# The first norm of a conditioned decoder trunk, by halves of the features

## The reference

```python
ada = jax.nn.silu(c) @ w_ada[l] + b_ada[l]
sh1, sc1, gt1, sh2, sc2, gt2 = jnp.split(ada[:, None, :], 6, axis=-1)
h = rmsnorm(x, norm1_g[l]) * (1.0 + sc1) + sh1
z = h @ w_in          # 1024 x 8192, then split into q, k, v, gates ...
```

## Time and profile before

| | us |
|---|---|
| median of 3 runs | 2022.48 |
| lowest and highest | 2020.64, 2023.28 |
| the profiled execution, its own time | 2021.04 |
| its span on the core | 2019.2 |
| TensorE busy in the span | 1995.1 |
| VectorE, ACT, POOL busy | 1158.5, 851.8, 183.2 |

### The profile page before, as it was taken

One profiled execution on the slowest core, in us unless ns is written; L12 is line 12 of the kernel. 1 busy time (PEld: TensorE's weight loads), 2 busy tenths in 40 slices (PEclk: granted clock), 3 DMA queues, 4 the chain that ended last, 5 costly groups with the idle time before them and its releaser, 6 DMA issues. The chain is left out here.

```text
span 2019.2 us, 35092 instructions
## 1 busy us (share of the span) xinstructions
PE 1995.1 (99%) x14624; PEld 1898.5 (94%) x14624; DVE 1158.5 (57%) x1814; ACT 851.8 (42%) x1155; POOL 183.2 (9%) x217
## 2 busy tenths in 40 slices
PE   6999999999999999999999999999999999999998
PEld 3879999999998999999989898999999999999998
DVE  5525566774446674646465455767735467646463
ACT  4124444665224244434431354456642333526252
POOL 0001120000032100000220011100000410000004
PEclk9999999999999999999999999999999999999999
DMA  9523243222253232323712314422222622322222
GB/s 362 188 75 108 91 160 97 77 82 86 83 210 145 84 123 87 136 84 126 275 64 69 110 65 145 130 85 81 82 83 84 250 69 84 105 70 99 84 90 105
DMA packets 79067, 233.91 MB, mean 116 GB/s; under 512 B 7376, under 2 KB 27856, under 8 KB 78544
## 3 DMA queue, kind: packets, MB, share of 16 engines
q1 hardware_dynamic: 57312, 206.99, 29.4%
q10 hardware_dynamic: 21616, 24.93, 3.8%
HBM read 219.80 MB, written 12.09 MB: 115 GB/s over the span
## 5 line engine op out<-in xcount | busy, mean ns | idle before, releaser
L1737 PE MATMUL acc<-h_hi,weight_h 128*128 128x288 f32 x1920 | 567.4, 298 | 0.0
L1737 PE MATMUL acc<-h_hi,weight_l 128*128 128x288 f32 x1920 | 560.3, 295 | 0.0
L1737 PE MATMUL acc<-h_lo,weight_h 128*128 128x288 f32 x1920 | 560.2, 294 | 0.0
L505 ACT ACTIVATE weight_h<-raw 128x1024 fp32r<-128x1024 f32 x188 | 199.2, 1060 | 609.9 <-PE acc L1737 513.1
L1737 PE MATMUL acc<-b_hi,weight_l 128*128 128x288 f32 x1520 | 429.5, 295 | 0.0
L1737 PE MATMUL acc<-b_hi,weight_h 128*128 128x288 f32 x1520 | 429.5, 295 | 0.0
L1737 PEld LDWEIGHTS acc<-h_hi,weight_h 128*128 128x128 f32 x1920 | 358.7, 188 | 5.3 <-issue 3.4
L1737 PEld LDWEIGHTS acc<-h_lo,weight_h 128*128 128x128 f32 x1920 | 358.5, 188 | 0.8
L1737 PEld LDWEIGHTS acc<-h_hi,weight_l 128*128 128x128 f32 x1920 | 358.4, 188 | 0.0
L1737 PE MATMUL acc<-b_lo,weight_h 128*128 128x288 f32 x1264 | 356.5, 294 | 0.0
L1068 DVE TENSOR_TENSOR weight_l<-raw,weight_h 128x1024 fp32r<-128x1024 f32 x176 | 227.3, 1292 | 224.1 <-ACT weight_h L505 223.6
(11 more groups left out here) (295 smaller groups left out, 3128.2 us busy)
## 6 DMA issues: line engine op xcount, KB each, us to landing
raw<-stream SPq DMA_DIRECT2D x290, 512.0 KB, 3.5
ada_raw<-ada_in SPq DMA_DIRECT2D x48, 512.0 KB, 6.4
first_raw<-ada_in SPq DMA_DIRECT2D x36, 512.0 KB, 14.5
s_s<-state_in ACTq DMA_DIRECT2D x8, 1024.0 KB, 6.8
ret_s_out<-s_s ACTq DMA_DIRECT2D x8, 1024.0 KB, 4.4
two_raw<-ada_in SPq DMA_DIRECT2D x12, 512.0 KB, 11.0
tables<-const_in SPq DMA_DIRECT2D x2, 1246.0 KB, 13.1
x<-x_in ACTq DMA_DIRECT2D x1, 2304.0 KB, 13.2
```

What stands on the lines that cost most here:

```text
L505: A(weight_h[:, j % 2, :], raw[:, (j + 2) % 4, :], ACT.Copy).then_inc(h_split, 1)
L1737: last = M(acc[j % 2][:, half, 0:HALF], w, r[:, k, half * HALF:(half + 1) * HALF], start=(k == order[0] and n == 0), stop=(k == order[-1] ...
```

## The change

- **x.** Its load moves from ACT's queue, where it was fourth, to the head of SP's queue, before the adaLN tiles.
- **Modulation groups by feature halves.** The host arranges the first sixteen adaLN tiles so that pair 0 holds shift and scale of features 0 to 511, and pair 1 those of features 512 to 1023. POOL writes both segments of a half in one operation. Groups 0 to 2 stay in the buffers that they had; the tiles of group 3 go to the unused slots of `weight_h` and `weight_l` (`early_raw`), since `h_lo` is written before they are used.
- **The norm by halves** (`first_norm`, `first_high`). VectorE multiplies x with the spread root first. ACT then makes `h_hi` as scale times it plus shift, and in a second pass the same sum unrounded into `tmp`; VectorE subtracts. The operations of the samples are split into two halves of the features each.
- **TensorE.** `first_mean` moves from the middle of group 1 into the middle of group 0 (behind its tile j = 1). `spread_root(0)` goes ahead of `turn(0)`. Group 3 and `turn(1)` move into `first_pair`: `on_high(0, 0)`, group 3 with `on_high(1, 0)` behind its first tile, the low parts of the first half for tile 0, `turn(1)`, the same for tile 1, then the second half, in which `on_high(1, 4, 2)` and `on_high(1, 6, 2)` take two feature tiles each. The number of matmuls is the same.

The diff, cut to its core:

```diff
@@ SP's queue
+            sp.dma_start(x[:], x_in).then_inc(x_loaded, 16)
             for n in range(ADA_PROLOGUE):
-                load_into(n, first_raw[n], first_loaded[n])
+                load_into(n, early_raw[n], first_loaded[n])
@@ ACT
-            act.dma_start(x[:], x_in).then_inc(x_loaded, 16)
...
+            def first_high(half):
+                act.wait_ge(ada_ready, half + 1 + 2)
+                if half:
+                    act.wait_ge(scales_ready, 1)
+                else:
+                    act.wait_ge(first_samples, GAINS_A)
+                for m in range(4 * half, 4 * half + 4):
+                    act.wait_ge(xn_ready, m + 1)
+                    A(prompt(one(h_hi, m)), prompt(one(tmp, m)), ACT.Identity, bias=column(ada, m), scale=column(scale1, m)).then_inc(h_rounded, 1)
+                for m in range(4 * half, 4 * half + 4):
+                    act.wait_ge(h_rounded, m + 1)
+                    A(prompt(one(tmp, m)), prompt(one(tmp, m)), ACT.Identity, bias=column(ada, m), scale=column(scale1, m)).then_inc(scaled, 1)
...
-                    act.wait_ge(scales_ready, 1)
-                    for m in range(KT):
-                        if m == 6:
-                            ada_row_out(1)
-                        scale_tile(m, scale1)
+                    first_high(0)
+                    ada_row_out(1)
                     ada_sum_out(1)
-                    act.wait_ge(ada_ready, 2 + 2)
-                    high(0, 0)
+                    first_high(1)
@@ VectorE
+                def scale_and_shift(half):
...
+                    dve.wait_ge(ada_ready, half + 1 + 2)
+                    gains_done, scaled_done = ((first_samples, GAINS_A), (first_samples, SCALED_A)) if half == 0 else ((scales_ready, 1), (s_scaled, 2))
+                    V.scalar_tensor_tensor(scale1[:, rows, :], ada[:, KT + 4 * half:KT + 4 * half + 4, :], 1.0, gb, ALU.add, ALU.mult).then_inc(gains_done[0], 1)
...
+                    V.tensor_tensor(cols(tmp), cols(tmp), of_half(scale1), ALU.mult).then_inc(scaled_done[0], 1)
...
+                    V.tensor_tensor(cols(h_hi), cols(tmp), of_half(ada[:, 0:KT, :]), ALU.add).then_inc(first_samples, 1)
...
+                    V.tensor_tensor(cols(tmp), cols(tmp), of_half(ada[:, 0:KT, :]), ALU.add).then_inc(sum_done[0], 1)
...
+                    last = V.tensor_tensor(samples(h_lo)[:, rows], samples(tmp)[:, rows], samples(h_hi)[:, rows].bitcast(F32), ALU.subtract)
...
+                def normal(half):
+                    for m in range(4 * half, 4 * half + 4):
+                        V.tensor_tensor(prompt(one(tmp, m)), prompt(one(x, m)), spread_p, ALU.mult).then_inc(xn_ready, 1)
+                def first_low(half):
+                    for m in range(4 * half, 4 * half + 4):
+                        dve.wait_ge(scaled, m + 1)
+                        V.tensor_tensor(prompt(one(h_lo, m)), prompt(one(tmp, m)), prompt(one(h_hi, m)).bitcast(F32), ALU.subtract).then_inc(h_ready, 1)
+                dve.wait_ge(spread, 1)
+                V.tensor_tensor(samples(tmp), samples(x), spread_s.unsqueeze(1).to_broadcast([128, KT, 2, HALF_S]), ALU.mult).then_inc(s_scaled, 1)
+                normal(0)
+                scale_and_shift(0)
+                normal(1)
+                first_low(0)
+                scale_and_shift(1)
+                first_low(1)
@@ POOL, add_bias
+                if p < 2:
+                    at_half = lambda t: t.rearrange("p (s h q) c -> p s h q c", s=2, h=2)[:, :, p, :, :]
...
+                    G.tensor_tensor(at_half(ada[:, 0:2 * KT, :]), ada_sum[:].rearrange("p (s q) c -> p s q c", s=2), at_half(both), ALU.add).then_inc(ada_ready, 1)
+                    return
@@ TensorE, first_pair
+                if n == 0:
+                    on_high(0, 0)
+                    ada_group(3, 0, early_raw[3], first_loaded[3], lambda: on_high(1, 0), 0)
+                    on_low(0, range(4))
+                    turn(1)
+                    on_low(1, range(4))
+                    on_high(0, 4)
+                    on_high(1, 4, 2)
+                    on_low(0, range(4, KT))
+                    on_high(1, 6, 2)
+                    on_low(1, range(4, KT))
+                    return
@@ TensorE, before first_pair
-                    ada_group(0, 0, first_raw[0], first_loaded[0])
-                    ada_group(1, 0, first_raw[1], first_loaded[1], first_mean)
+                    ada_group(0, 0, first_raw[0], first_loaded[0], first_mean)
+                    ada_group(1, 0, first_raw[1], first_loaded[1])
+                    spread_root(0)
                     turn(0)
-                    spread_root(0)
                     ada_group(2, 0, first_raw[2], first_loaded[2])
-                    ada_group(3, 0, first_raw[3], first_loaded[3])
-                    turn(1)
@@ the host
+    by_half = [w_ada[0][seg][4 * half:4 * half + 4] for half in range(2) for seg in range(2)]
+    w_ada = np.concatenate(by_half + [w_ada[l][seg] for l, seg in ADA_ORDER[2:]])
```

More of the change, by code:

```diff
@@ L50 @@
 ADA_SUMMED = (0, 1, 4, 10)
+GAINS_A, SCALED_A, HIGH_A, SUM_A, HIGH_B = range(1, 6)
 NORM_SHIFT = [ADA_ORDER.index(pair) + 1 for pair in ((0, 0), (0, 3), (1, 0), (1, 3))]
@@ L192, in build @@
                                  for g, home in ((1, "b_hi"), (2, "b_lo"), (3, "h_lo"), (4, "h_hi"))]
+        early_raw = first_raw[0:3] + [[place(f"early_raw{q}", [128, 1024], F32, offs[home] + slot * 4096)
+                                       for q, (home, slot) in enumerate((("weight_h", 2), ("weight_h", 3), ("weight_l", 2), ("weight_l", 3)))]]
         x_part = place("x_part", [128, 2, NB_S], F32, offs["side"] + 4608)
@@ L1085, in shift_samples @@
             def shift_samples(n, shift_at):
-                if n == 0:
-                    V.tensor_tensor(by_sample(h_hi), by_sample(tmp), to_samples(ada[:, shift_at:shift_at + KT, :]), ALU.add).then_inc(first_samples, 1)
-                    dve.wait_ge(first_samples, 1)
                 V.tensor_tensor(by_sample(tmp), by_sample(tmp), to_samples(ada[:, shift_at:shift_at + KT, :]), ALU.add).then_inc(xn_ready, 1)
             def low(n, shift_at):
[L1094 to L1098, removed]
+                dve.wait_ge(h_rounded, rounded(n))
                 V.tensor_tensor(samples(h_lo), samples(tmp), samples(h_hi).bitcast(F32), ALU.subtract).then_inc(h_ready, 1)
@@ L1136, in _ @@
                     root(0)
[L1137 to L1140, removed]
+                    first_norm()
                     dve.wait_ge(tables_loaded, 16)
@@ L1779, in first_mean @@
             def first_mean():
+                pe.wait_ge(const_loaded, 16)
                 pe.wait_ge(squares_ready, 1)
@@ L1791, in first_pair, with on_high @@
                 pe.wait_ge(acc_free, lay * LAYER_TILES + off + 2)
-                def on_high(j, first):
-                    for k in range(first, first + KT // 2):
+                def on_high(j, first, count=KT // 2):
+                    for k in range(first, first + count):
                         if j == 0:
                             pe.wait_ge(h_rounded, rounded(n) + k)
-                        if n == 0 and k == 0:
-                            pe.wait_ge(first_samples, 1)
+                        if n == 0 and j == 0 and k % 4 == 0:
+                            pe.wait_ge(first_samples, (HIGH_A, HIGH_B)[k // 4])
                         for w in (weight_h, weight_l):
@@ L1802, in on_high, with on_low @@
                                 M(acc[j][:, half, 0:HALF], w[:, j, k * 128:(k + 1) * 128], h_hi[:, k, half * HALF:(half + 1) * HALF], start=(k == 0 and w is weight_h), stop=False)
-                def on_low(j):
-                    for k in range(KT):
+                def on_low(j, steps=range(KT)):
+                    for k in steps:
                         if j == 0:
@@ L1810, in on_low @@
                             last = M(acc[j][:, half, 0:HALF], weight_h[:, j, k * 128:(k + 1) * 128], h_lo[:, k, half * HALF:(half + 1) * HALF], start=False, stop=(k == KT - 1))
-                    last.then_inc(tile_done, 1)
+                    if k == KT - 1:
+                        last.then_inc(tile_done, 1)
+                if n == 0:
[10 more added lines that the diff above has]
+                    return
                 on_high(0, 0)
@@ L1821, in _, with ada_group @@
             for lay in range(DEPTH):
-                def ada_group(n, loads, slots=ada_raw, loaded=ada_loaded, between=None):
+                def ada_group(n, loads, slots=ada_raw, loaded=ada_loaded, between=None, after=1):
                     p, odd = n // 2, n % 2
@@ L1834, in ada_group @@
                         last.then_inc(ada_used, 1)
-                        if j == 1 and between is not None:
+                        if j == after and between is not None:
                             between()
```

31 lines of the change are left out of this document (23 added, 8 removed).

## The result

Before 2022.09 us (22 runs, 2020.64 to 2024.34), after 2025.65 us (22 runs, 2024.98 to 2026.88): ratio 1.0018, interval [1.0012, 1.0024]. The change makes the kernel 3.6 us slower, clear of the noise and less than the 0.2% that I called telling. The forecast was 2023.2, in a range of 2019.3 to 2026.0. The profiled executions differ by more, 2019.2 and 2023.6 us of span: 4.4 us.

What follows compares the result with a forecast made beforehand. TensorE, 99% busy, was taken as the bound from tile 2 on, so prologue moves carry to the end: 2021.04 + 0.75 = 2021.8, by the median 2023.2 us; range 2019.3 to 2026.0.

Steps and rivals of the forecast that it cites:

- x is early, and it helps nothing: Start: x is there by 8.7 us, 7 us earlier, but the squares end at 17.9, only 0.8 us earlier.
- ACT's queue is held by turns: Start: queues alternate by packet, so c arrives about 8.5 us and `small` about 9.9 instead of 7.0, bounds 7.0 to 10.9.
- The mean: TensorE's mean matmuls: start at 17.9 us, partly at 1.2 GHz, take 6.05 us, end at 23.95 instead of 26.12.
- rival (E): Mean ends at 25.6 us, from `small` at 10.9 and 5.4 us at 1.2 GHz: +2.4 us, 2024.9; chance 0.12.
- (D): Start: `small` lands at 13.2 us or later, ACT's queue getting still fewer turns; loss passes 4 us; chance 0.04.
- The path from e: From the mean's end to tile 0's end: 23.45 us, so tile 0 ends at 47.4 us against 46.66.
- The hand-over: Between tile 0's end and tile 2: only 16 matmuls cover preparing `weight_l`, so TensorE idles 1.8 us.
- The order of group 3: In `first_pair`: the last adaLN tile waits for `on_high(1, 0)`, so the second turn comes 4 us later.
- rival (C): Clock falls to 1.2 GHz in a pause from e+6.5 to e+18.2: +4 to +11 us, 2027 to 2033; chance 0.05.
- The sum: Whole kernel: tile 2 starts at 51.4 instead of 50.64 us, +0.75 us, giving 2021.8, by the median 2023.2 us.
- my offset of 1.44 us: Whole kernel: profiled execution 2021.04 us against median 2022.48; the difference is added to the forecast.
- (A): Start: ACT's queue isn't held up, `small` lands at 7.0 us, e at 21.1: -2.1 us, 2020.4; chance 0.2.

Runs made afterwards that it cites:

- the run with the warm start: The changed kernel with 16 matmuls of constants between `const` and the mean, where TensorE idled: 2023.44 us, ratio 1.0006 against the kernel before.

## Why the prediction was right, point by point

As in the forecast, e is the end of the mean.

- **x is early, and it helps nothing.** Right. x lay ready for 7.5 us. Three runs show that the setup chain is what stood before the squares: letting c and `small` pass, or the squares, gives back all of the loss; moving x alone in the kernel before gives 0.0.
- **ACT's queue is held by turns.** The mechanism was right, the size too small. By the queues' packets in the changed kernel, from 4 to 6 us and from 6 to 8 us:

```profile
q1 hardware_dynamic: 46, 0.85, 100.5%
q10 hardware_dynamic: 5, 0.00, 0.3%
```

```profile
q1 hardware_dynamic: 46, 0.85, 98.7%
q10 hardware_dynamic: 45, 0.01, 2.7%
```

Turns are one for one, 46 to 45, but only from about 6 us on: c's first packets come 2 us later than I had them. c landed at 9.6, behind x, and `small` was read at 11.31, not 9.9 and past my bound of 10.9. The Trainium skill's account (DMA: Bandwidth & Descriptors, "Queues, rings and completion order"), a whole packet of some 9 to 17 descriptors before a switch, fits the first window, where x has the queues almost to itself, and not the second: there 18 KB elements and 288-byte ones alternate one by one. By it c would have come after all of x; c did land after x, but 45 of its 128 packets had gone beside x's from 6 to 8 us, and the rest of the delay is the late first packet. Why that one is late no run here shows. The 10.9 for `small` that I had worked out from the page was nearer to the 11.31 than my own 9.9.
- **The mean.** From 17.9 I had 6.05 us; it took 6.03 from 19.40, and the run with the warm start shows that its length is the clock. e was 25.43 instead of 23.95, all of it from `small`. That is the e of rival (E), 25.6, which made +2.4 us by my path; the chance that I gave it was 0.12. The whole loss, +4.4 by the profiles, lies past (E), and not by the cause that (D) names, `small` at 13.2: my path behind e was too short too.
- **The path from e.** Named rightly in every step, and 2.35 us too short: tile 0's last low part ended at 51.23, e + 25.8, not e + 23.45. ACT's tiles with scale and shift took 2.93 us for four, 0.73 each, where I had taken 0.63 from eight in 5.02: 0.3 us in the first half, 0.7 in the second (5.75 us for the eight instead of 5.04). And group 3's tiles took 0.98 us for tile 12 (35.86 to 36.84) instead of 0.43, 1.84 for three instead of 1.3, 1.1 us together. The 0.43 was half of a pair. One tile alone takes 1.05 us with its tail (4 records from 35.86) and two 1.06 (8 records from 25.36), as the four matmuls of two tiles in a row write four different strips of 32 rows of `misc` and start within 0.1 us of each other; three take 1.91 and four 1.92. Cutting group 3 behind its first tile left two tiles alone, the first and the last. That is 2.1 of the 2.35; the rest is spread over the other steps.
- **The hand-over.** Right: TensorE waited 1.7 us for `weight_l` of tile 2, 1.8 forecast, and one run without the split's wait took 1.35 us off.
- **The order of group 3**, "4 us later" for the second turn, was 7.4 us (43.2 against 35.8 for its end), as e and the pace above came on top; ahead, it gives 1.8, in part because its pairs stay together.
- **The clock's fall, rival (C).** I gave it 0.05 for the changed kernel, on the ground that the kernel before kept its clock over a pause of 1.66 us. It does so only in some executions. The Trainium skill (TensorE: Matmul & The Clock Gate, "What's actually happening") has the clock drop after idleness. The trace agrees that a pause comes first, of 1.66 us here; behind a pause of the same length the granted clock stayed at 1.00 in two other profiles. In the profile of the changed kernel no fall occurs behind the mean.
- **The sum.** By the profiles +4.4 against +0.75: 1.5 from `small`, 2.35 from the path, less 0.2 where tile 2 followed tile 0's end faster. By the medians +3.56, since the profile of the kernel before was an execution with a kept clock, 1 us below its median; my offset of 1.44 us was added to both alike and could not see that. Here luck helped: 4.4 us on 2021.04 with that offset make 2026.9, past the range; the changed kernel's median lies only 0.25 us above its profile. The ends of the range were also misadded: 1.1 us beyond (A) and (E), where the text says 1.3. The direction, the chain through `small`, the length of the mean and the hand-over were right for the reasons given; the sizes of `small`'s delay and of the path behind e were not, and the wide range covered them.

What stays open: why c's first packet comes at 6 us, and how the 22 runs of the changed kernel divide by their clock; only one of them was profiled. The mean granted clock of each is a hint: nine have 0.997 and a median of 2026.17 us, twelve 0.998 and 2025.49. The run with group 3 ahead shows what could lie behind such 0.7 us, a fall in the pause ahead of the mean, with which the mean took 6.71 us instead of 6.03; that the nine had it is not shown. In the kernel before, times and mean clock don't go together.

## What to carry to other kernels

Before a transfer is moved to the head of a queue, list what the other queue still has to bring and what stands in program order before the first use: here 164 KB of small parameters were worth more than 2.3 MB of tokens. Put work on early data ahead of work on late data on each engine; that alone gave 4.2 us. When work is cut in halves so that it can start early, look at what each half leaves as cover for the next weight preparation, and at the tiles of the second half that now queue behind the first. Before a group of matmuls is cut, see which of them run side by side: here a tile alone took as long as two.

## What the runs showed of the hardware that was not expected

- Matmuls of constants in a pause of TensorE made the kernel faster, 2025.65 to 2023.44 us, as the clock rose from 1.2 to 2.4 GHz during them and not within the mean (16 matmuls in 6.03 us, then in 4.10). Five of them in another pause raised nothing: the granted clock stayed at 0.50 for 4.6 us behind them.
- The same kernel had its clock fall for about 3 us behind a pause of 1.66 us in one profile and keep it in two others; with a late rise in the mean (6.10 us instead of 4.10) that makes 1.9 us between two executions, half of the 3.7 us over which its runs spread.
- A queue's first small packets were seen 2 us later beside 18 KB packets of the other queue (about 6 us) than beside 4 KB ones, and from then on the queues alternated one element to one.
- adaLN matmuls that write different strips of 32 rows of one PSUM tile ran side by side: one 512 KB tile took 1.05 us, two in a row 1.06, three 1.91, four 1.92.
- The mean granted clock of a stretch read 1.00 at the start of a trace while matmuls had the durations of 1.2 GHz (739 ns against 406 in the mean).
